# A pooled and gated two-block network on one core: the gather of an expert's tokens is done for two experts at a time, and three pieces of work ahead of it change places

## The reference, cut to what matters

```python
cond = silu(c)
mod = cond @ w_mod + b_mod
sh1, sc1, g1, sh2, sc2, g2 = split(mod, 6)
h = layer_norm(x) * (1 + sc1) + sh1
y = token_mixer(h, ...)       # z = h @ w_in; conv of 31 taps; spatial gating; w_a, w_b, w_out
x = layer_norm(alpha * x + g1 * y, post1_g, post1_b)
h = layer_norm(x) * (1 + sc2) + sh2

logits = h @ w_router + b_router
top_logits, top_idx = top_k(logits, 4)
top_w = softmax(top_logits)
for each expert e:            # the tokens that chose it
    gate, up = split(h[tokens of e] @ w_gu[e] + b_gu[e], 2)
    gate = minimum(gate, 7.0); up = clip(up, -7.0, 7.0)
    act = (up + 1) * (gate * sigmoid(1.702 * gate))
    y[tokens of e] += (act @ w_dn[e] + b_dn[e]) * top_w
x = layer_norm(alpha * x + g2 * y, post2_g, post2_b)
```

## Time and profile before

| | us |
|---|---|
| median of 3 runs | 2382.03 |
| the runs | 2389.56, 2382.03, 2376.08 |
| the profiled execution | 2388.37 |
| its span, first to last instruction | 2386.7 |
| PE busy | 2125.1 |
| DVE busy | 859.9 |
| ACT busy | 432.8 |

### The profile page before, as it was taken

The page is one execution under the profiler, slowest core; times in us unless marked ns, Lnnn a source line. Parts: engine busy times, 40 slices in busy tenths (PEclk is TensorE's granted clock), DMA queues, the critical chain, the costliest instruction groups (busy, mean ns, idle before and its releaser), DMA issues. The chain is left out here.

```text
span 2386.7 us, 30911 instructions
## 1 busy us (share of the span) xinstructions
PE 2125.1 (89%) x11317; PEld 1358.5 (57%) x11318; DVE 859.9 (36%) x1418; ACT 432.8 (18%) x503; POOL 61.0 (3%) x126
## 2 busy tenths in 40 slices
PE   5998995989999999899999889789988977778997
PEld 3776674434444444344444334459978866656986
DVE  1395117111111111111121111456556754644654
ACT  1010001000000010000010000125433421213541
POOL 2000002000000000000000000100000000000000
PEclk8999796899999999999999999889998977888999
DMA  9446642649999999599999549345554400114552
GB/s 363 155 143 242 222 157 88 242 188 407 422 422 422 422 422 422 230 422 422 422 422 409 231 191 396 142 149 185 187 190 129 137 1 1 53 53 133 190 184 81
DMA packets 142574, 578.66 MB, mean 242 GB/s; under 512 B 10522, under 2 KB 12042, under 8 KB 93260
## 3 DMA queue, kind: packets, MB, share of 16 engines
q1 hardware_dynamic: 135824, 563.12, 60.8%
q0 software_dynamic: 3552, 12.61, 1.6%
q10 hardware_dynamic: 3131, 1.98, 0.3%
HBM read 576.62 MB, written 1.05 MB: 242 GB/s over the span
## 5 line engine op out<-in xcount | busy, mean ns | idle before, releaser
L982 PE MATMUL bank<-ring,area 128*64 128x512 f32 x2304 | 511.1, 602 | 0.0
L982 PEld LDWEIGHTS bank<-ring,area 128*64 128x64 f32 x2304 | 169.3, 139 | 322.3 <-issue 316.8
L212 DVE TENSOR_TENSOR ring_r<-ring,ring_r 128x2048 fp32r<-128x2048 f32 x92 | 210.9, 2292 | 207.3 <-ACT ring_r L209 206.4
L707 PE MATMUL bank<-area,ring 128*128 128x256 f32 x1024 | 229.2, 388 | 9.9 <-issue 8.0
L707 PEld LDWEIGHTS bank<-area,ring 128*128 128x128 f32 x1024 | 199.7, 195 | 39.3 <-issue 9.2
L209 ACT ACTIVATE ring_r<-ring 128x2048 fp32r<-128x2048 f32 x92 | 175.9, 1913 | 232.5 <-PE bank L744 207.7
L1860 DVE TENSOR_SCALAR area<-bank 128x512 f32<-128x512 f32 x36 | 24.9, 692 | 508.7 <-PE bank L982 508.7
L741 PE MATMUL bank<-area_r,ring_r 128*128 128x256 f32 x704 | 202.0, 287 | 2.2 <-DVE area_r L1727 2.2
L743 PE MATMUL bank<-area_r,ring_r 128*128 128x256 f32 x704 | 200.5, 285 | 0.0
L744 PE MATMUL bank<-area_r,ring_r 128*128 128x256 f32 x704 | 200.5, 285 | 0.0
L963 PEld LDWEIGHTS bank<-area 128*128 128x128 f32 x1184 | 139.3, 197 | 32.0 <-DVE area L1861 24.2
(11 more groups left out here) (294 smaller groups left out, 2015.3 us busy)
## 6 DMA issues: line engine op xcount, KB each, us to landing
ring<-in_w_gu SPq DMA_DIRECT2D x256, 1024.0 KB, 13.9
ring<-in_w_dn SPq DMA_DIRECT2D x64, 1024.0 KB, 10.7
area<-in_w_dn SPq DMA_DIRECT2D x64, 1024.0 KB, 12.3
ring<-in_mlp_w SPq DMA_DIRECT2D x64, 1024.0 KB, 5.4
ring<-in_w_mod SPq DMA_DIRECT2D x24, 1024.0 KB, 8.7
ring<-in_w_in SPq DMA_DIRECT2D x24, 1024.0 KB, 6.2
ring<-in_gdn_w_in SPq DMA_DIRECT2D x16, 1024.0 KB, 5.5
ring<-in_ple_gate_w SPq DMA_DIRECT2D x8, 1024.0 KB, 8.0
```

Of the source, the lines that this page charges most:

```text
L212: nc.vector.tensor_tensor(unit_low(i), raw, unit_high(i), ALU.subtract).then_inc(w_split, 1)
L707: ins = mm(bank(g)[:, m * S:(m + 1) * S], u[k // UK][:, k % UK, c:c + P], xT[:, k, :], start=k == 0, stop=k == ND - 1)
L982: ins = mm(bk[hf * BLK:(hf + 1) * BLK, :], x[:, kt, :], eslot[kt][:, c:c + BANK], start=False, stop=kt == ND - 1)
```

## The change

- **Gather in pairs.** Experts are taken in groups of four (`EG`), and the loop's body is written out four times, so that PE, DVE and ACT go round it 8 times. `slots` holds the 0/1 matrices of four experts, two side by side, and `xg` the gathered tokens of two pairs. In each expert's block PE gathers half of the features (4 of 8 tiles) of both experts of the pair to come: 8 products of 128 columns in place of 16 of 64 (`gather_pair`). DVE finds the slots three experts ahead in place of one. Overflow blocks still gather 64 columns for themselves.
- **Modulation between slabs.** The 16 units of `mod2` are listed, and multiplied, in four portions of 4, each ahead of one slab of `u` and `g_a`; only the transposes of the modulation rows stay behind `g_b`.
- **Early bias split.** The split of `b_gu` is done in pieces behind the evictions of `w_b` and of the first half of `w_a`. Its areas move (`bgu_raw`, `bgu_res`, `bgu_tmp`), and POOL issues its load when the convolution's and the mixing's banks are empty, in place of `w_b`'s.
- **Routing.** Most DVE steps are done for both tiles of tokens at once; the gates go straight to `gate_of`, the places straight to `place`; the two clears stand ahead of the logits; the exponentials are asked for ahead of the selection; the copies of g2 and of the gates' transpose, and PE's product with `b_dn`, stand behind the first gather.

```diff
-        add("u", slabs(w_in, range(2 * C, 3 * C)))
-        add("g_a", slabs(w_in, range(4 * C, 5 * C)))
+        mod2_halves = fours(w_mod, (4, 8))
+        for i, (name, c) in enumerate((("u", 2 * C), ("u", 2 * C + 1), ("g_a", 4 * C), ("g_a", 4 * C + 1))):
+            add(f"mod2_{i}", mod2_halves[4 * i:4 * i + 4])
+            add(f"{name}_{c % C}", slabs(w_in, (c,)))
         add("g_b", slabs(w_in, range(5 * C, 6 * C)))
-        add("mod2", fours(w_mod, (4, 8)))
...
-            with eng.Fori(0, NE) as e:
-                n_tok = eng.value_load(counts[0:1, bass.ds(e, 1)], min_val=0, max_val=S)
...
+            with eng.Fori(0, NE // EG) as g:
+                for j in range(EG):
+                    n_tok = eng.value_load(counts[0:1, bass.ds(g * EG + j, 1)], min_val=0, max_val=S)
...
-            feature_major("u", "u", hT, C)
-            feature_major("g_a", "g_a", hT, C)
+            for i, (name, s) in enumerate((("u", 0), ("u", 1), ("g_a", 0), ("g_a", 1))):
+                modulation_half("mod2", first_unit[f"mod2_{i}"], i // 2, i % 2)
+                feature_major(f"{name}_{s}", name, hT, 1, first=s)
             feature_major("g_b", "g_b", hT, C)
-            modulation("mod2", 2)
+            modulation_rows("mod2", 2)
...
+            def gather_pair(bk, p, dh):
+
+                for d in range(UK):
+                    for t in range(NT):
+                        ins = mm(bk[:, d * P:(d + 1) * P], h2_tok[:, t, (UK * dh + d) * P:(UK * dh + d + 1) * P],
+                                 slots[:, p, t, :], start=t == 0, stop=t == NT - 1)
+                step(ins)
...
             def last_block(w):
-                e = w[0]
+                j = w[1]
                 DV.started(pe, w)
-                gate_and_up(e, xg, True)
+                gate_and_up(w, xg[:, j // 2, :, j % 2 * BLK:(j % 2 + 1) * BLK], True)
                 AC.started(pe, w)
                 scatter(spread_T, y_blk).then_inc(w_used, 1)
                 DV.did(pe, w, "next_slots1")
-                gather(slots)
+                gather_pair(bX, 1 - j // 2, j % 2)
...
+            def bias_thirds(r, hf):
+
+                ps, cs = slice(NE * r, NE * (r + 1)), slice(hf * 1024, (hf + 1) * 1024)
+                src = bgu_raw[ps, cs]
+                for i in range(r):
+                    link(v.tensor_copy(bgu_tmp[ps, 0:1024], src))
+                    link(v.tensor_tensor(bgu_res[ps, cs], src, bgu_tmp[ps, 0:1024], ALU.subtract))
+                    src = bgu_res[ps, cs]
+                link(v.tensor_copy(bgu_parts[ps, cs], src))
...
                     empties(ins, g)
+                    if nm == "w_b" or q < 2:
+                        if nm == "w_b" and q == 0:
+                            dve.wait_ge(late_in, 64)
+                        k = q if nm == "w_b" else 4 + q
+                        bias_thirds(k // 2, k % 2)
```

More of the change, by code:

```diff
@@ L20 @@
 SPLITS = 3
+EG = 4
 KCH = 64
@@ L865, in _ @@
             pe.wait_ge(cond_ready, 1)
-            modulation("mod1", 1)
+            for kq in range(2):
+                modulation_half("mod1", first_unit["mod1"] + 4 * kq, 0, kq)
+            modulation_rows("mod1", 1)
             to_features("hT", tok(2), xn_ready, 0)
@@ L948, in _ @@
             emptied(pe, G("pos"))
-            for i in range(4):
-                t, hf = i // NH, i % NH
-                ins = mm(banks[i][:, :], gateT[:, t * P:(t + 1) * P], b_dn_sb[:, hf * BANK:(hf + 1) * BANK],
-                         start=True, stop=False)
-            ins.then_inc(moe_pe, 1)
             bX, bG, bU, bT = banks[4], banks[5], banks[6], banks[7]
@@ L1040, in _ @@
             pe.wait_ge(moe_dve, 1)
-            gather(slots)
+            assert all(G("g2_bc", q) % BANKS not in (4, 6) for q in range(2)) and G("gateT") % BANKS not in (4, 6)
+            for dh in range(2):
+                gather_pair((bX, bU)[dh], 0, dh)
+            emptied(pe, G("gateT"))
+            for q in range(2):
+                emptied(pe, G("g2_bc", q))
+            pe.wait_ge(route_ready, 4)
+            pe.wait_ge(bgu_ready, 1)
+            for i in range(4):
+                t, hf = i // NH, i % NH
+                ins = mm(banks[i][:, :], gateT[:, t * P:(t + 1) * P], b_dn_sb[:, hf * BANK:(hf + 1) * BANK],
+                         start=True, stop=False)
+            step(ins)
             def overflow(w):
@@ L1327, in _, with pairs @@
             empties(f(mod_row[:, 0, :], bank(g)[:, :], ACT.Copy), g)
-            def pairs(gname, fn):
-                for q in range(4):
+            def pairs(gname, fn, qs=range(4)):
+                for q in qs:
                     g = G(gname, q)
@@ L1800, in _ @@
[L1800 to L1811 removed]
+                n[0] += 1
```

245 lines of the change are left out of this document (120 added, 125 removed).

## The result

| | before | after |
|---|---|---|
| median, us | 2380.62 | 2416.56 |
| the four runs | 2376.08 to 2389.56 | 2413.18 to 2424.51 |
| the profiled execution's span | 2386.7 | 2422.8 |
| ratio, 95% interval | | 1.0151, 1.0112 to 1.0191 |

The forecast was 2331 us, its range 2312 to 2358: it named the wrong sign. Both profiled executions lie at the upper end of their kernel's runs, so the spans can be compared as they stand: 36.1 us longer. Two points divide that: the loop's first bias product, and ACT's last sigmoid.

The account below looks back on a forecast made before the run. PE was taken to set the pace, with the DMA close behind in the expert loop. Gains of 14.9 + 7.5 + 29 = 51.4 us led from 2388.4 to 2337.0 profiled, 2331 as a median, range 2312 to 2358.

Parts of the forecast that it names:

- What bounds the kernel: Expert loop: PE sets the pace at 28.87 us an expert, the DMA needs 29.84 us; overflow blocks drain its queue.
- Modulation between slabs: Ahead of the loop: modulation portions between slabs make PE wait for no weights; -14.9 us, bounds -14.9 and 0.
- Early bias split: Ahead of the loop: 16 us of DVE work leave the path, fit into eviction gaps and cost nothing.
- Routing: Router to loop: earlier logits, fewer selection steps, earlier first gather; -7.5 us, bounds 0 and -14.
- rival (e): Mixing and first gather may run at full clock without the modulation's waits: 6 to 13 us more, 2320; chance 0.12.
- Gather in pairs: Expert loop: 1.9 us saved per expert, partly lost where the DMA paces; net -29 us, ends -24 and -34.
- rival (a): Expert loop: one jump per expert misses its target, 4.6 us each; 2452 us profiled, 2446 median; chance 0.06.
- (b): Expert loop: only the jump back misses, 37 us, a third of it absorbed, so +24: 2355 us; chance 0.12.
- The price of a miss: Expert loop: a jump whose target isn't held costs what a small load takes to land, 4.6 us.
- The Trainium skill's rule: Instruction fetch: PE holds 128 KiB, 2048 instructions, and a jump outside what is held stalls.

## Why the prediction was wrong, point by point

- **What bounds the kernel**: right. TensorE and, close behind it, the DMA with 29.84 us an expert by my count; 29.82 was measured in two kernels, and there the landing times stood at 26 to 27 us for "near 25". One reading was off without an effect on the sum: the sigmoid at 1412 us is 31.3 us from the next, not "some 33 us or more", and others than the four named are over 33; the overflow blocks do lie where the text says.
- **Modulation between slabs**, -14.9: right: 14.1 of the 14.95 us in the profile, and alone 15 to 28 us between medians. That run's profile, 17.9 us shorter than before, has 19.5 ahead of the loop, 8.9 around the loop's overflow blocks, and 10.5 more in the second block.
- **Early bias split**, no cost: right. The router's product starts 15.2 us earlier, which the modulation explains.
- **Routing**, -7.5, bounds 0 and -14: the size was off. The loop's first product came 32.0 us earlier, of which 17.1 remain here. The order of events was as said, the count started 5.9 us behind the router as computed, but the first gather and the product with `b_dn` ran at full clock (7.5 us for 14.3); the term was taken at half clock, with full clock as its bound and as a part of rival (e). The other part of (e) did not come: from the modulation's transposes to the end of the router's product it took 150.0 us for 150.3, so the mixing ran as before. The remaining 3 us are a shorter count and entry.
- **Gather in pairs**, -29: here it failed, with +50.8 us measured in the loop. The gather itself was as said: 2.05 us for 1.9 (0.128 us a product; for the bound of 0.09 there is no row), 26.5 us an expert for 27.0, experts at TensorE's pace behind an overflow and then at the DMA's. The loop with two copies took 1033.0 us for 1067.8. That these 34.8 us come near the 29 is in part luck: 21.6 of them are there without any pair, and the pairs add 13.2. The near hit of its total is luck of the same kind: some 11 us more ahead of the loop and 6 more in it than forecast, and a second block 9 us longer, which had no term. In the changed kernel the term failed because it was summed as if the body of some 2350 instructions were held, and that assumption had no row behind it. The text says so in rival (a): "Nothing before shows whether 9 blocks can be". The runs show that it isn't: 73 blocks fetched in 900 us, jumps of 6 us, and 109 us lost in the loop of before by four copies alone. The text then gave (a) 0.06 and (b) 0.12 on the ground that straight code fetches without idle time in the earlier trace rows. That row was no evidence: it shows fetches in sequence, which run ahead; behind a jump back to code that isn't held the fetch starts only after the jump (3.4 to 3.6 us after its start in the changed kernel).
- **The price of a miss**, 4.6 us from the smallest load's landing: for the jump back 5.9 to 6.2 us beside the weights, 3.3 to 3.8 without. Two misses follow each other at a turn's start, which neither rival had; (a) counted one per expert and (b) one per turn; (b)'s 2355 us was too low by 62. By chance (a)'s sum of 31.6 us an expert is the turn's mean, 31.5. Its 2452 us profiled (2424.5 measured) were too much by 35 in the loop, where turns with an overflow lost less, by 9.6 ahead of it, and too little by 17 behind it.
- **The Trainium skill's rule** stood in the text: by it "the new body just fails to fit". It was the only source that spoke to a body of this length at all, and a sentence that no trace contradicted should have weighed more than silence. As a number it is not exact here: by 2048 the body of 1792 would still have been held.

## What to carry to other kernels

Count the instructions of a loop's body on each engine, code that is mostly jumped over included, before writing it out more often: up to 1600, a straight loop on TensorE was held here, and at 1792 it was fetched anew in each pass. With some 2350 and beside a stream of weights that cost about 19 us a turn, against which stood 8 us of gain. If unrolling is wanted for double buffers, as here, take the smallest factor and pay with a copy on an idle engine; with two copies the whole change gave 2.4%, of which the work ahead of the loop alone gives 1.9, where with four copies it lost 1.5%. And when an engine's idle time is put down to another one, look whether that one had itself been waiting for the first one's sequencer.

## What the runs showed of the hardware

- A taken branch to held code takes 0.21 us on TensorE's sequencer. A loop's jump back to code that isn't held took 3.3 to 3.8 us with idle DMA queues, 4.5 to 5.2 beside half of the weights (213 GB/s over a turn), 5.9 to 6.2 beside all of them (415 GB/s). The block's transfer takes about 1 us in each case; what grows is the wait for its start, 1.0, 2.8 and 3.6 us in the median. A missed jump right behind another took 2.2 to 2.7, 4.9 to 6.0, and 6.2 to 7.2 us (4.5 to 4.7 in the kernel before written out four times).
- The sequencer ran 3.9 us of products ahead in the loops and 4.3 us in the changed kernel: one miss of 3.8 us vanished there, two in a row left 3.2 us of idle time in the loops and 12.1 us in the kernel.
- The shortest body that wasn't held, 1792 instructions, is not fetched in part: nine fetches of 256 instructions in each pass.
- After a stop of 12 us the next gate and up starts at 1.2 GHz (a granted clock of 0.50 from 563.3 to 568.3 us, 1.00 behind it) and takes 16.08 us for 13.91: a stall costs more than its own length.
